# State-space scan on one core: the products that spread the decay rows, summed over all 128 partitions in place of 48

## The reference, cut to what matters

```python
a_cum = jnp.cumsum(A, axis=-1)                       # A = dt * a, one value per token and head
seg = a_cum[..., :, None] - a_cum[..., None, :]
decay = jnp.exp(jnp.where(tri, seg, -jnp.inf))       # source token s, target token l >= s
cb = jnp.einsum('bclgn,bcsgn->bcgls', Cc, Bc)
y_diag = jnp.einsum('bcgls,bgecls,bcsgep->bclgep', cb, decay, X)
```

## Time and profile before

| | before |
|---|---|
| median of 3 runs | 1333.81 us (1333.57 to 1334.62) |
| the profiled execution's own time | 1333.94 us |
| its span | 1332.2 us |
| mean granted TensorE clock over the span | 0.931 of full |
| TensorE busy | 1153.7 us, 87% of the span |
| VectorE, ScalarE, GpSimd busy | 622.5, 438.8, 78.1 us |

### The profile page before, as it was taken

How to read it: one execution, slowest core, us unless ns; L and a number is a source line. 1 busy time by engine, 2 the same in 40 slices (tenths; PEclk the granted TensorE clock), 3 DMA queues, 4 the chain that set the end, 5 groups by cost and what they waited for, 6 DMA issues and landing times.

```text
span 1332.2 us, 19419 instructions
## 1 busy us (share of the span) xinstructions
PE 1153.7 (87%) x8137; PEld 858.6 (64%) x8137; DVE 622.5 (47%) x1173; ACT 438.8 (33%) x807; POOL 78.1 (6%) x118
## 2 busy tenths in 40 slices
PE   5899989998987757699999675679999999999988
PEld 2677748886842213169984231236999878999856
DVE  3554884546540102056753020115993456555574
ACT  3636533231320000034332000003545554433473
POOL 3000223531000000000000000000000000000000
PEclk9899998999998788699999888879999979999899
DMA  9837864318789999995778999998353303554100
GB/s 328 313 127 255 314 221 160 106 48 323 312 346 422 422 420 420 419 370 190 299 296 345 421 421 421 421 413 310 127 190 127 127 1 127 190 186 157 53 1 32
DMA packets 104187, 339.17 MB, mean 255 GB/s; under 512 B 7849, under 2 KB 10774, under 8 KB 81574
## 3 DMA queue, kind: packets, MB, share of 16 engines
q1 hardware_dynamic: 97408, 334.51, 65.0%
q10 hardware_dynamic: 6694, 3.43, 1.0%
HBM read 336.88 MB, written 1.05 MB: 254 GB/s over the span
## 4 chain that ended last, share of the span: by engine, by line
PE 63%; DMA 12%; SPq 11%; DVE 9%; ACT 3%; issue 2%; ACTq 0%; DVEq 0%
PE bank L708 8%; PE bank L710 8%; PE bank L709 8%; SPq L1402 7%; DMA weight_ring<-in_w_up_dram 5%; PE bank L1061 4%; SPq L1413 3%; PE bank L610 3%; DMA arena<-in_w_up_dram 3%; DMA arena<-in_w_gate_dram 3%; DVE arena L2119 2%; PE bank L1255 2%; PE bank L850 2%; PE bank L687 2%; PE bank L688 2%; DMA weight_ring<-in_ada_w_dram 2%
## 5 line engine op out<-in xcount | busy, mean ns | idle before, releaser
L2119 DVE TENSOR_TENSOR weights_low<-weight_ring,weights_high 128x1024 fp32r<-128x1024 f32 x142 | 173.7, 1224 | 146.2 <-ACT weights_high L1584 145.8
L1584 ACT ACTIVATE weights_high<-weight_ring 128x1024 fp32r<-128x1024 f32 x142 | 149.8, 1057 | 189.7 <-PE bank L710 175.3
L708 PE MATMUL bank<-input_high,weights_high 128*128 128x272 f32 (+1 forms) x672 | 197.1, 293 | 6.6 <-DVE input_low L2119 4.2
L710 PE MATMUL bank<-input_high,weights_low 128*128 128x272 f32 (+1 forms) x672 | 193.4, 288 | 0.0
L709 PE MATMUL bank<-input_low,weights_high 128*128 128x272 f32 (+1 forms) x672 | 193.2, 288 | 0.0
L708 PEld LDWEIGHTS bank<-input_high,weights_high 128*128 128x128 f32 x672 | 128.3, 191 | 10.7 <-issue 6.8
L2119 DVE TENSOR_TENSOR arena<-arena,bank 128x512 f32<-128x512 f32 (+1 forms) x38 | 24.6, 651 | 231.9 <-PE bank L1061 211.4
L710 PEld LDWEIGHTS bank<-input_high,weights_low 128*128 128x128 f32 x672 | 128.5, 191 | 0.0
L709 PEld LDWEIGHTS bank<-input_low,weights_high 128*128 128x128 f32 x672 | 128.2, 191 | 0.1
L1061 PE MATMUL bank<-weight_ring,arena 128*32 128x512 f32 x448 | 64.5, 720 | 31.5 <-DMA weight_ring<-in_w_up_dram 18.7
L1061 PE MATMUL bank<-arena 128*32 128x512 f32 x384 | 54.4, 709 | 26.1 <-DMA arena<-in_w_up_dram 17.5
(11 more groups left out here) (462 smaller groups left out, 2092.0 us busy)
## 6 DMA issues: line engine op xcount, KB each, us to landing
weight_ring<-in_ada_w_dram SPq DMA_DIRECT2D x24, 2048.0 KB, 9.1
weight_ring<-in_w_gate_dram SPq DMA_DIRECT2D x16, 2048.0 KB, 25.4
arena<-in_w_down_dram SPq DMA_DIRECT2D x16, 2048.0 KB, 32.7
arena<-in_w_gate_dram SPq DMA_DIRECT2D x12, 2048.0 KB, 21.2
arena<-in_w_up_dram SPq DMA_DIRECT2D x12, 2048.0 KB, 33.0
weight_ring<-in_w_up_dram SPq DMA_DIRECT2D x12, 2048.0 KB, 27.7
weight_ring<-in_even_w_in_dram SPq DMA_DIRECT2D x9, 2048.0 KB, 9.2
expert_slots<-in_w_up_dram SPq DMA_DIRECT2D x8, 2048.0 KB, 32.6
```

What stands on the lines that cost most here:

```text
L708: pe.matmul(b[:, 0:width], hi[:, k, :], high[:, k, t0:t0 + width], start=k == 0, stop=False)
L710: mm = pe.matmul(b[:, 0:width], lo[:, k, :], high[:, k, t0:t0 + width], start=False, stop=k == KD - 1)
L1584: act.activation(WHI[:, j % 2], quarter_of(j), ACT.Copy).then_inc(weights_high, 1)
L2119: return dve.tensor_tensor(out_, a, b, op)
```

## The change

The products of `decay_args` take all 128 rows of PICK and CUMT in place of the first 48. For that the 80 other rows must hold zeros: VectorE clears both tiles once, behind the clearing of ADT and ahead of the writing of PICK, and waits for these two before it goes on. The number of instructions on TensorE, their columns, and what they compute stay the same.

```diff
             def decay_args(h):
                 b = s_open()
-                pick = PICK[0:SELROWS, h:h + 1]
+                pick = PICK[:, h:h + 1]
                 for i, ((t0, r), (c0, w)) in enumerate(zip(SRC, SSD_COLS)):
-                    pe.matmul(b[0:r, c0:c0 + w], pick.broadcast_to([SELROWS, r]), CUMT[0:SELROWS, t0:L2], start=i == 0, stop=False)
+                    pe.matmul(b[0:r, c0:c0 + w], pick.broadcast_to([P, r]), CUMT[:, t0:L2], start=i == 0, stop=False)
...
             dve.memset(ADT, 0.0)
+            dve.memset(CUMT[:, :].bitcast(F32), 0.0)
+            then(dve.memset(PICK[:, :].bitcast(F32), 0.0))
             tt(PICK[0:SELROWS, :], ident[0:SELROWS, 0:SSD_H], ident[0:SELROWS, 32:SELROWS], ADD)
```

## The result

| | before | after |
|---|---|---|
| median of 5 runs each | 1333.81 us (1329.65 to 1336.04) | 1323.51 us (1322.95 to 1325.31) |
| ratio of the runs, 95% interval | | 0.9941 [0.9913, 0.9968] |
| the profiled execution's own time | 1333.94 us | 1325.31 us |
| its span | 1332.2 us | 1323.6 us |
| mean granted clock over the span | 0.931 | 0.939 |

The change makes the kernel faster, by more than the forecast and outside its range. Median against median it is 10.3 us, where 6.1 were forecast; between the two profiled executions it is 8.6. The profiled execution of after is the slowest of its five.

What follows compares the result with a forecast made beforehand. TensorE's order bounds the stage, its clock on the path. Savings of 0.9 ahead of the scan, 4.4 in it and 0.9 in the norm, 6.2 us, take 1333.94 to 1327.7 us; eight-in-ten range 1326.0 to 1334.3.

Steps and rivals of the forecast that it cites:

- main step: Scan stage on TensorE: array use, rows included, sets the clock; 128 rows, 31% more full-array columns a pair, keep 2.4 GHz.
- the weight loads: The 48 products of L1206: wider rows could show only in load length, 0.3 us lost at most, taken as 0.
- the last layer: Clock falls from 1258.7 to 1265.4 may shift; 1.5 us allowed either way.
- ahead of the scan: Fourth `decay_args` to first `scan_out`, with the clock kept at 2.4 GHz: 0.9 us saved, bounds 0.4 to 1.0.
- scan: Loop of `scan_out` and `decay_args` at 2.4 GHz: 22.13 us becomes 17.7, saving 4.4, bounds 3.9 to 5.0.
- first norm: First norm products L1227 behind the scan: 1.83 us in place of 2.71, 0.9 saved.
- starts at the old distances: Sign expected in the profile after: L1206's products start as far apart as before, with weight loads under 190 ns.
- the memsets: Two VectorE memsets and a wait at 1005.8, 0.46 us, covered by 0.86 idle: cost 0, at most 0.5.
- The wait ahead of the last `scan_out`: New wait of 0.6 us in the last turn, for the multiplication behind the last `decay_args`; counted in the scan.
- 0.4 + 0.16: Ahead of the scan: four transposes faster at 2.4 GHz, 0.4 us, and VectorE's idle behind its first drain gone, 0.16.
- the slower rival: A 1.7 us pause ahead of the scan drops the clock, all eight pairs slow: 5.3 us slower, 1339.2 us; 13%.
- both falls gone: The forecast case: clock falls at about 1057 and 1074 both vanish; 60%, own range 1326.0 to 1330.0 us.

Runs made afterwards that it cites:

- before_look: The kernel before, unchanged, profiled a second time in one single execution: 1325.04 us.
- i_cols48: Kernel after with `decay_args` products back on 48 rows, and its narrow tiles (third product, small mask product) at 128 columns: 1333.73 us, ratio 1.0033 to before.
- b_behind_mask: Kernel after with 128 rows only for the nine heads whose `decay_args` follows another `decay_args`, the other seven at 48: 1322.84 us, ratio 0.9939 to before.
- a_behind_scan: Kernel after with 128 rows only for seven heads (0 and the even ones from 4), the other nine at 48: 1326.19 us, ratio 0.9963 to before.
- e48_clear: Kernel after with its two memsets and wait kept, but all `decay_args` products back at 48 rows: 1331.28 us, ratio 0.9987 to before.
- before_look2: The kernel before, unchanged, profiled a third time in one single execution: 1326.76 us.
- f_full_tile: Kernel after with every product of `decay_args`, the small mask product included, made a full 128 x 128 tile: 1321.66 us, ratio 0.9913 to before.
- h_f_and_e: Kernel after with full 128 x 128 tiles in `decay_args` and `scan_out`'s products for the last 16 sources over 128 rows: 1321.53 us, ratio 0.9936 to before.
- d_mask128: Kernel after with the small mask product L1207 over 128 rows in place of 16: 1324.77 us, ratio 0.9945 to before.

## Why the prediction was wrong

Its main step held and its clock terms add up to what was measured; the step that failed is the second gain, the weight loads, priced at nothing and worth 1.5 us. With that term the forecast would have been 1326.2, and the last layer and a spread that it didn't know of make up the rest (point 6). The sum between the profiled executions, by pieces, where the undisturbed 48-row stage (before_look: 8.13, 17.91, 2.03) parts the clock from the rest:

| | forecast | measured | of it the clock | of it the loads |
|---|---|---|---|---|
| up to the first `decay_args` | 0 | +0.6 | | |
| ahead of the scan | -0.9 | -1.80 | -1.22 | -0.58 |
| scan | -4.4 | -5.13 | -4.22 | -0.91 |
| first norm | -0.9 | -0.68 | -0.68 | |
| rest, with the last layer | 0 (1.5 either way) | -1.6 | | |
| sum | -6.2 | -8.6 | -6.1 | -1.5 |

1. **"I conclude that how much of the array is used matters, rows included."** Right for the rows of `decay_args`. The clearing alone does nothing, 64 rows are as good for the clock as 128, wider tiles without the rows give nothing, and 1 of 74 runs against 69 of 99 is above 1330. That it is the share of the whole array, and not these rows as such, isn't shown: no run raises the share by columns alone as far as by rows (i_cols48 widens only products of 16 columns). The clock's part came to 6.1 us against a forecast of 6.2. There is some luck in that: it is 0.3 more than forecast ahead of the scan (point 5), 0.2 less in the scan, and 0.2 less in the first norm, which takes 2.03 us at 2.4 GHz, where I had taken the 1.83 of the second. The Trainium skill (TensorE: Matmul & The Clock Gate, Part 1) lets the clock go by how busy the engine has been; the earlier trace rows and i_cols48, busy for 6.00 of 6.00 us at 0.50, show that a busy engine isn't enough here.

2. **"A wider contraction could only show in weight loads ... I take 0, as the loads lie beside the products before them." This is the step that failed.** I priced the length of a load and took for granted that it lay beside the product ahead. The first load of L1206 did not: behind L1209 the engine had waited for it. In the chain that wait stood in the 0.39 to 0.40 of L1206, which I read as the cost of its three products; with the load early they take 0.20 or 0.21, and L1209 keeps its 0.21 to 0.22. TensorE's timeline shows both, first of before, then of after:

```profile
1068.58 0.28 PE L1209 MATMUL bank<-arena 128*128 128x256 bf16 x1
1068.79 0.47 PE L1206 MATMUL bank<-decay_rows,head_picks 48*128 48x272 f32 x3
```

```profile
1056.20 0.28 PE L1209 MATMUL bank<-arena 128*128 128x256 bf16 x1
1056.24 0.45 PE L1206 MATMUL bank<-decay_rows,head_picks 128*128 128x272 f32 x3
```

   A piece of the chain runs from the end of the record before it to its own end, and not from start to start: L1209's record of 1068.58 ends at 1068.86, where a piece of 0.40 of L1206 begins. By starts, the distance from L1209 to L1206 was 0.21 and is 0.04, so the sign "starts at the old distances" failed too.

   Nine short `decay_args` at 0.19 are 1.7 us; the pieces show 1.5, for the reason in point 4. The bound that I gave had only a loss in it (0.3 us) and no gain. b_behind_mask against a_behind_scan shows the same with the clock at 1.00 in both: 7.55 and 16.95 against 8.12 and 17.89, 1.5 us. Their medians are 3.35 us apart, of which this explains less than half; the profiled executions, 1323.22 and 1322.78, are only 0.4 apart, and the rest stays open. The other cost in this part, the memsets, came as forecast: VectorE's idle time ahead of the next split went from 0.86 to 0.37, and the split still waited for ScalarE.

3. **The last layer.** I allowed 1.5 either way and it gave 1.6. The rest of the span takes one of three values in the 14 profiles: 241.25 to 241.34, 241.87 to 242.01, and 242.78 to 242.85. The middle one goes with one fall of 3.4 us, somewhere between 1257.3 and 1270.5, the lowest with one of 6.8, and the highest (before and e48_clear) with two falls. before_look2, with 48 rows, has the lowest. So it goes with where the falls lie on the last layer's work, and the lowest value doesn't need the rows. What places them wasn't tried.

4. **The wait ahead of the last `scan_out`.** Forecast 0.6. The timeline of TensorE shows it as the idle time in brackets, in before_look, where the clock alone is undisturbed, and then in after:

```profile
1078.23 1.14 PE L1218 MATMUL bank<-arena 128*64 128x272 f32 x12 [0.63 <-DVE arena L2119]
```

```profile
1079.17 0.92 PE L1218 MATMUL bank<-arena 128*64 128x272 f32 x8 [0.83 <-DVE arena L2119]
```

   Right for the clock's part. The other 0.20 is what the hidden load of the last short `decay_args` gives back, since this wait hangs on the head before it: six short ones in the scan at 0.19 are 1.14, less 0.20 is 0.94, and the table has 0.91. With 0.63 the undisturbed scan was 17.91, where the forecast had 17.7.

5. **The piece ahead of the scan.** The clock's part is 1.22 where I had 0.9. The fourth `decay_args` gave the 0.36; from its end to the first `scan_out` it was 6.15 us before (1058.36 to 1064.51) and 5.28 in before_look (1056.19 to 1061.47), which is 0.87 where I had 0.4 + 0.16. The 0.4 came (the first drain is 0.48 behind that `decay_args`, and was 0.89). What was too small is the 0.16: the six drains took 4.13 us from the first start to the last end, and take 3.67 in before_look, 0.61 each, so the 0.66 that I took for VectorE's own pace was not its pace at 2.4 GHz. The pause was forecast at 1.7 and is 1.22 on TensorE (in the chain 1.12 "issue", from 1062.20). That it wouldn't make the clock fall was the open point of the slower rival, 1339.2 us; the clock stayed at 1.00, in all nine profiles with wider rows.

6. **The reference point.** The forecast took the profiled execution of before, which lay at its median, as the kernel's steady behaviour. It is one draw of a kernel that takes between 1324.7 and 1336.6 us, and before_look, 1325.04 us, shows that "both falls gone" is a state that the kernel before reaches by itself at times. What the change does to the clock is to make that state the usual one. So the gain on the median depends on how often before falls: 11.95 us for f_full_tile where before had 1333.61, 6.54 for h_f_and_e, with the same time, where before had 1328.07. Why the groups of runs differ in that wasn't found. Of the 4.2 us between 1327.7 and 1323.5, 2.4 are the profiled sums (8.6 against 6.2: the loads 1.5, the last layer 1.6, ahead of the stage 0.6 the other way; the clock's part is 0.1 less than forecast), and 1.8 are the distance of after's profiled execution, 1325.31, to its median.

7. **The rest of the kernel.** This stage is a small part of what the clock costs. By the mean granted clock, 0.931 and 0.939, about 184 us of before's span and 161 of after's ran at 1.2 GHz (an estimate, twice what is missing to 1.00, times the span); the two falls of this stage are 17 of them. The others, nearly all ahead of the stage, are in all 14 profiles, and no edit here was aimed at them.

## What to carry to other kernels

Where the granted clock of a busy TensorE falls, look at how many rows of the array its products fill: rows of zeros cost no time here (a scan of 17.88 us with 64 rows, 17.91 with 48 where the clock stayed) and kept it at 2.4 GHz. Where small products stand between large ones, look in the timeline at when each weight load begins against the product ahead, not at how long it is; giving neighbours the same full tile shape hid the loads here (a `decay_args` from 0.71 over 0.52 to 0.42 us). And take a second profile of the kernel before, or the spread of its runs, before sizing a clock effect from one: the mode of that one execution may not be the kernel's.

## What the runs showed of the hardware that was not expected

- A weight load began together with the product ahead when both used 128 rows and 128 columns (L1206 behind L1209, 1056.20 both), and 0.21 to 0.22 us later with 48 or 64 rows. With 128 rows and 16 columns in the neighbour (L1207 in d_mask128) the load behind it still stood 0.10 later. Within `scan_out` 128 x 64 tiles behind one another were enough: 0.93 against 1.07 us. The rule behind it wasn't worked out.
- The same instructions were run at 1.00 or at 0.50 in different executions: the scan of the kernel before took 22.13, 17.91 and 19.24 us in three profiles.
- The start of the stage itself moves by up to 4.9 us between the profiles of all kernels (1050.86 to 1055.77), which is as much as most of the effects here, and by 1.8 us between the three of the kernel before (1053.34 to 1055.16).
